# Nine of twelve modulation chunks multiplied and folded by GpSimd, with TensorE summing them over partitions

## What is computed

```python
mod = jax.nn.silu(c) @ w_ada[l] + b_ada[l]              # c: 1 x 1024, w_ada: 1024 x 6144
sh1, sc1, g1, sh2, sc2, g2 = jnp.split(mod, N_MOD, axis=-1)
h = layer_norm(x) * (1.0 + sc1[:, None]) + sh1[:, None]
x = layer_norm(ALPHA * x + g1[:, None] * mix, ln1_g[l], ln1_b[l])
```

## Time and profile before

| | |
|---|---|
| median of 3 runs | 2429.97 us (2426.4 to 2431.11) |
| the profiled execution | 2420.81 us, span 2418.7 us |
| TensorE busy | 2067.4 us (85%) |
| VectorE busy | 1560.9 us (65%) |
| ScalarE busy | 1184.9 us (49%) |
| GpSimd busy | 809.6 us (33%) |
| mean granted clock of TensorE | 0.91 |
| chain that ended last | TensorE 50%, DMA 24%, VectorE 12%, ScalarE 7%, issue 5%, GpSimd 3% |

### The profile page before, as it was taken

The page is one execution under the profiler, slowest core; times in us unless marked ns, Lnnn a source line. Parts: engine busy times, 40 slices in busy tenths (PEclk is TensorE's granted clock), DMA queues, the critical chain, the costliest instruction groups (busy, mean ns, idle before and its releaser), DMA issues.

```text
span 2418.7 us, 34343 instructions
## 1 busy us (share of the span) xinstructions
PE 2067.4 (85%) x13020; PEld 1579.0 (65%) x13020; DVE 1560.9 (65%) x3481; ACT 1184.9 (49%) x2367; POOL 809.6 (33%) x684
## 2 busy tenths in 40 slices
PE   6989998887697886666669899787998899989998
PEld 4445576776555555555567788656887657858863
DVE  5565665698875677788566776567766536854422
ACT  1123332466556667666676567756776740111110
POOL 2000000465743334455544896323433320700000
PEclk9999889999798998666679999988999999999999
DMA  4321235788899999999999999999999986353431
GB/s 170 122 96 70 72 139 210 284 325 315 336 366 410 414 418 415 420 421 421 418 416 415 402 356 416 415 417 412 413 413 411 411 311 226 114 191 108 171 139 70
DMA packets 162132, 729.71 MB, mean 302 GB/s; under 512 B 10160, under 2 KB 13360, under 8 KB 95920
## 3 DMA queue, kind: packets, MB, share of 16 engines
q0 software_dynamic: 73728, 536.90, 55.0%
q1 hardware_dynamic: 88240, 190.62, 21.7%
HBM read 725.38 MB, written 2.10 MB: 301 GB/s over the span
## 4 chain that ended last, share of the span: by engine, by line
PE 50%; DMA 24%; DVE 12%; ACT 7%; issue 5%; POOL 3%; SPq 0%; DVEq 0%; POOLq 0%; ACTq 0%
DMA AR<-in_uv,C 19%; PE PA L925 14%; PE PD L1514 8%; PE PA L1444 5%; PE PD L925 5%; PE PA L1457 3%; ACT AR L2032 3%; DMA WR<-in_w_up 2%; DMA WR<-in_w_down 2%; DVE AR L2892 2%; PE PA L1598 2%; PE PD L1598 2%; PE PA L1283 1%; PE PA L1296 1%; PE PA L1391 1%
## 5 line engine op out<-in xcount | busy, mean ns | idle before, releaser
L2892 DVE CUSTOM_DVE_ANT_0 AR<-AR,HN 128x1024 f32<-128x1024 f32 x467 | 591.6, 1271 | 366.3 <-issue 192.7
L3186 POOL DMA_INDIRECT AR<-in_uv,C x467 | 573.9, 1229 | 725.1 <-PE PD L1514 672.1
L1514 PE MATMUL PD<-C,AR 128*128 128x128 f32 x3736 | 586.7, 310 | 222.4 <-ACT AR L2032 220.7
L1514 PEld LDWEIGHTS PD<-C,AR 128*128 128x128 f32 x3736 | 497.7, 160 | 351.6 <-ACT AR L2032 301.5
L2032 ACT ACTIVATE AR<-AR,SC 128x1024 f32<-128x1024 f32 x467 | 536.6, 1149 | 15.2
L2028 ACT ACTIVATE SC<-SC 128x1 f32<-128x1 f32 x512 | 103.5, 202 | 406.9 <-DVE SC L2892 406.1
L3186 POOL DMA_INDIRECT WR<-in_uv,C x45 | 54.0, 1200 | 464.0 <-DVE C L2640 394.4
L1444 PE MATMUL PA<-HT,WR 128*128 128x256 f32 x704 | 167.6, 385 | 9.5 <-DMA WR<-in_w_up 9.5
L925 PE MATMUL PA<-HT,WR 128*128 128x256 f32 (+1 forms) x544 | 170.9, 475 | 0.0
L925 PE MATMUL PA<-AR,WR 128*128 128x256 f32 (+1 forms) x896 | 170.0, 352 | 0.7 <-ACT AR L1817 0.7
L925 PEld LDWEIGHTS PA<-AR,WR 128*128 128x128 f32 x896 | 152.2, 193 | 17.7 <-ACT AR L1817 1.1
(11 more groups left out here) (495 smaller groups left out, 3085.3 us busy)
## 6 DMA issues: line engine op xcount, KB each, us to landing
WR<-in_w_up SPq DMA_DIRECT2D x22, 2048.0 KB, 15.6
WR<-in_w_in SPq DMA_DIRECT2D x18, 2048.0 KB, 12.5
WR<-in_w_ada SPq DMA_DIRECT2D x12, 2048.0 KB, 8.1
WR<-in_w_down SPq DMA_DIRECT2D x9, 2048.0 KB, 9.2
WR<-in_w_pq SPq DMA_DIRECT2D x8, 2048.0 KB, 18.8
WR<-in_w_o SPq DMA_DIRECT2D x4, 2048.0 KB, 18.4
WR<-in_w_out SPq DMA_DIRECT2D x4, 2048.0 KB, 19.0
AR<-in_uv,C POOLq DMA_INDIRECT x467, 14.6
```

The lines of the kernel that those rows point to most:

```text
L1514: ins = nc.tensor.matmul(acc[i // 4][:, P * (i % 4):P * (i % 4) + P], uv_row(j, D + P * i, D + P * i + P), ident, start=(k == 0 and i % 4 ...
L2892: ttr(uv_row(j, 0, D), uv_row(j, 0, D), HN[:, t, :], 1.0, 0.0, ALU.mult, ALU.add, DOT[:, j:j + 1]).then_inc(s["dots"], 1)
L3186: nc.gpsimd.indirect_dma_start(uv_row(ring_slot(turn), 0, 2 * D), None, uv, bass.IndirectOffsetOnAxis(ap=IDX[:, t % 2, i:i + 1], axis=0),) ...
```

## The change

Chunks 3 to 11 leave TensorE's `modulation_rows`. GpSimd waits for each chunk's load, multiplies it in place with `csil2` (repeated over the 512 columns), folds its 8 blocks to 4, 2 and 1 by three sums, the last into `ADAROW[i]`, and counts `ada`. TensorE's `modulation_columns(i)` waits for `ada` and sums over all 128 partitions by a column of ones, again 4 products. Columns of chunks 2, 3 and 4 stand where rows 3 and 4 were, those of 5 to 8 together after the second `head_sums`, ahead of `rhat`; 9, 10 and 11 stay. `ADAROW` gets places in X for chunks 3 to 8. The nine chunks alternate between slots 0 and 1, each load waiting for GpSimd's last sum on that slot; the halves of `w_o` use slots 2 and 1. `down_part` gives 8 steps in 3 rows in place of 3 a row, and the turn of `xn3` goes ahead of the first `in2` products.

```diff
+def down_part(row):
+    at = [min(max(8 * (row + i - DOWN_FROM) // 3, 0), DOWN_IN_ROWS) for i in (0, 1)]
+    return range(at[0], at[1])
...
-        ADAROW = [HN[:, 2 + i % 2, 512:1024] for i in range(12)]
+        ADAROW = ([HN[:, 2 + i % 2, 512:1024] for i in range(3)]
+                  + [X[:, i // 2, 512 * (i % 2):512 * (i % 2) + 512] for i in range(6)]
+                  + [HN[:, i, 512:1024] for i in range(1, 4)])
...
-            col_chunk(w_ada, 512 * i, 512, "a", ada_job(i))
-        SLOTS += [0, 1, 0, 1, 2, 0, 1, 2, 0]
-        col_chunk(w_o, 0, 512, "d", FIRST_D[("wo", 0)])
-        col_chunk(w_o, 512, 512, "a", FIRST_A[("last", 7)])
+            col_chunk(w_ada, 512 * i, 512, "ada", i - 3)
+        SLOTS += [0, 1, 0, 1, 0, 1, 0, 1, 0]
+        col_chunk(w_o, 0, 512, "a", FIRST_A[("last", 7)])
+        col_chunk(w_o, 512, 512, "d", FIRST_D[("wo", 0)] + 1)
...
-        SLOTS += [1, 2, 0, 3, 1, 0, 1]
+        SLOTS += [2, 1, 0, 3, 1, 0, 1]
...
+                    elif chan == "ada":
+                        sp.wait_ge(s["ada"], job + 1)
...
-                pe.wait_ge(s["a_free"], ada_job(i) + 1)
+                if i < 3:
+                    pe.wait_ge(s["a_free"], ada_job(i) + 1)
+                else:
+                    pe.wait_ge(s["ada"], i - 2)
                 b = bank("a")
                 for m in range(4):
-                    ins = nc.tensor.matmul(b[:, m:m + 1], ADAROW[i][:, P * m:P * m + P], cc("sel")[:, 0:1],
+                    ins = nc.tensor.matmul(b[:, m:m + 1], ADAROW[i][:, P * m:P * m + P],
+                                           cc("sel" if i < 3 else "ones")[:, 0:1],
                                            start=True, stop=True)
...
-            for i in (3, 4):
-                modulation_rows(i)
-                modulation_columns(i - 1)
+            for i in (2, 3, 4):
+                modulation_columns(i)
...
             head_sums()
-            modulation_columns(4)
+            for i in range(5, 9):
+                modulation_columns(i)
             pe.wait_ge(s["rhat"], 2)
...
-                if lev > 1:
-                    modulation_columns(lev + 3)
...
-                modulation_rows(lev + 4)
...
-            modulation_rows(10)
             modulation_columns(10)
-            modulation_rows(11)
...
-                for c in part(r, DOWN_FROM, 3, DOWN_IN_ROWS):
+                for c in down_part(r):
...
+            turn_block("xn3", 3, "dd")
             pe.wait_ge(s["a_free"], FIRST_A["xn3_2"] + 2)
...
-            turn_block("xn3", 3, "dd")
             pe.wait_ge(s["d_free"], FIRST_D["in2"])
...
+            pool.wait_ge(s["cleared"], 1)
+            pool.wait_ge(s["csil"], 1)
+            for i in range(3, 12):
+                number = CNUM["ada3"] + i - 3
+                pool.wait_ge(w_sem[SLOTS[number]], 16 * (len(EARLIER[number]) + 1))
+                z = HOME[SLOTS[number]].rearrange("p (k n) -> p k n", k=KD)
+                joined(tt_(z, z, csil2.unsqueeze(2).broadcast_to([P, KD, 512]), ALU.mult), "mod")
+                joined(tt_(z[:, 0:4, :], z[:, 0:4, :], z[:, 4:8, :], ALU.add), "mod")
+                joined(tt_(z[:, 0:2, :], z[:, 0:2, :], z[:, 2:4, :], ALU.add), "mod")
+                if i >= 9:
+                    pool.wait_ge(s["a_full"], FIRST_A["ada0"] + 1)
+                joined(tt_(ADAROW[i], z[:, 0, :], z[:, 1, :], ALU.add), "ada")
```

More of the change, by code:

```diff
@@ L180 @@
     ("hT", 4, 4), ("pm", 4, 4), ("ada_pm", 1, 0), ("cT", 3, 2), ("q", 4, 4), ("kv", 4, 4), ("qkT", 16, 8), ("ada_qk", 2, 0),
-    ("att", 38, 64), ("pr", 2, 0), ("ada0", 4, 0), ("lora", 12, 0), ("tok", 4, 0), ("ada1", 1, 0), ("kn", 0, 5), ("bonus", 0, 1),
+    ("att", 38, 64), ("pr", 2, 0), ("ada0", 3, 0), ("lora", 12, 0), ("tok", 4, 0), ("ada1", 4, 0), ("kn", 0, 5), ("bonus", 0, 1),
 ]:
@@ L194 @@
         jobs("a", ("mt", _lev))
-    if _lev > 1:
-        jobs("a", ("columns", _lev + 3))
     jobs("d", ("right", _lev, 0), 2)
@@ L204 @@
         jobs("a", ("kk", 0))
-    jobs("a", ("rows", _lev + 4))
 jobs("a", ("left", LEVELS - 1, 0))
@@ L211 @@
 jobs("d", ("state", 0))
-jobs("a", ("rows", 10))
 jobs("a", ("columns", 10))
-jobs("a", ("rows", 11))
 for _c in range(1, NT):
@@ L386, in ada_job @@
 def ada_job(i):
-    if i >= 5:
-        return FIRST_A[("rows", i)]
-    return (FIRST_A["ada_pm"], FIRST_A["qkT"] + 6, FIRST_A["ada_qk"], FIRST_A["ada0"], FIRST_A["ada0"] + 2)[i]
+    return (FIRST_A["ada_pm"], FIRST_A["qkT"] + 6, FIRST_A["ada_qk"])[i]
 def in2_job(b):
@@ L498, in build @@
                  "xn", "xn2", "xn3", "xn4",
-                 "row_half", "ct_b", "ct_p", "e_full", "e_free", "mats", "ynorm", "ycomb_p", "cn", "qk_normed", "masked", "smax", "probs", "raw_used", "lora_in", "prt",
+                 "ada", "mod", "row_half", "ct_b", "ct_p", "e_full", "e_free", "mats", "ynorm", "ycomb_p", "cn", "qk_normed", "masked", "smax", "probs", "raw_used", "lora_in", "prt",
                  "kx_sq", "kr", "rkk", "rexp", "rhat", "khat", "cleared",
@@ L943, in modulation_rows @@
             def modulation_rows(i):
-                w = chunk(pe, CNUM["ada0"] if i == 0 else CNUM["ada1"] + i - 1 if i < 3 else CNUM["ada3"] + i - 3)
+                w = chunk(pe, CNUM["ada0"] if i == 0 else CNUM["ada1"] + i - 1)
                 b = bank("a")
```

## The result

| | before | after |
|---|---|---|
| median of 4 runs each, same chip | 2428.18 us (2423.57 to 2431.11) | 2506.62 us (2498.27 to 2507.68) |
| profiled execution, span | 2420.81, 2418.7 us | 2506.52, 2504.1 us |
| first gather | 428.81 us | 502.51 us |
| GpSimd busy | 809.6 us | 956.7 us |
| TensorE busy, mean granted clock | 2067.4 us, 0.91 | 2070.7 us, 0.89 |

The ratio is 1.0319, 95% interval 1.0295 to 1.0344: 78 us slower.

A forecast was written before the change was run, and what follows sets the result against it. Prologue to the first gather bounds the kernel, TensorE leading from 320 us, but VectorE's earlier stretch decides this change: 80 - 9.4 + 2 - 2.9 = +70 us, profiled 2491, forecast 2500 on the runs' median; range 2445 to 2520.

The forecast's parts named there:

- The hold of VectorE: From the last mix at 263 us, VectorE's SBUF operations take turns with GpSimd's whole instructions: 80 us later.
- no turn at all: Bound where VectorE stands until GpSimd ends at 357 us, then works alone: 94 late, less 6, so 88 us.
- GpSimd's prices: Per chunk on GpSimd: product 7.1 us, sums 4.6, 2.38 and 1.28, with joins 15.7 us; nine chunks 141 us.
- Attention: Attention's VectorE steps read PSUM or are one element wide, so should be nearly free of the hold.
- the third rival: Attention's one-element operations are held too by chunks 4 and 5: up to +20, 2519 us; inside the forecast's 0.70.
- Columns 5 to 8 together: Four column products on TensorE ahead of `rhat`: cost 0 to 3.3 us, taken as 2.
- The levels: Rows and columns taken from TensorE in the level stretch, from the first `left` to `y`: 9.4 us gained.
- Rows of chunks 10 and 11: Removing them from TensorE gives nothing, since the first turned tile waits for VectorE's output norm, ending at 388.1 us.
- The end: Turn of the last tile ahead of the first `in2` products, so the second ones start earlier: 2.9 us gained.
- The `down` steps and the `w_o` halves: Spreading 76 `down` steps over 28.5 rows: nothing, give or take 1 us; swapping the `w_o` halves: nothing.
- Rival 1: GpSimd's work hides and VectorE loses under 10 us: 2430 - 14 = 2416 us; chance 0.13.
- rival 2: VectorE wins every meeting, GpSimd delays `rhat` about 30 us: +20, 2450; chance 0.13 including what lies between it and forecast.

The follow-up runs named there:

- the version with four chunks: Before, with GpSimd taking only chunks 3 to 6, TensorE keeping chunks 7 to 11, and the turn of the last normed tile moved: 2438.5 us, ratio 1.0044.
- second filler run: After, with 11 useless products spread over four groups of 32 output partitions ahead of the columns of chunk 10, and again of chunk 11: 2496.8 us, ratio 1.0303.
- the extra GpSimd work: Before, with 25 two-input GpSimd operations added on idle space from near 231 us, and one late VectorE wait for their end: 2458.7 us, ratio 1.0134.
- both versions: The version with four chunks (2438.5 us), and before with GpSimd taking only chunks 3 and 4 after a wait for attention's mixes (2421.5 us, ratio 0.9985).
- both filler runs: After with useless products ahead of the columns of chunks 10 and 11: all in one group of output partitions 2506.5 us, spread over four 2496.8 us.

## Why the prediction was right, step by step

The forecast was 2500 and 2506.6 came; the mechanism was the forecast one. Up to the first gather the sum was 80 + 2 - 9.4 = 72.6, and 73.7 was measured. That the two are so close is in part luck, since several terms were off and cancel:

- **The hold of VectorE: 80 taken (81 by the walk), 74.1 in the trace,** of which 2.6 are already there at 150 us, ahead of anything that differs. So the term was some 8.5 us too large. The step that failed is "VectorE gets one instruction or a short run at a time": it gets exactly one. I let GpSimd pay for nearly all of VectorE's 23 us; VectorE got only 24 instructions in, and they cost GpSimd 0.3 us or less each. GpSimd's last 24 instructions took 95.3 us and ended at 360.7, not 380, and VectorE's remaining 13.6 us came behind. The bound that I had named for "no turn at all" (88) has the same form, and lay on the other side.
- **GpSimd's prices held.** The product took 7.02 us (7.1 forecast), the sums 4.50, 2.34 and 1.26 (4.6, 2.38, 1.28). The Trainium skill's single price (GPSIMD Engine Reference, "Performance versus the Vector engine"), by which I had estimated 8.9 us for the product, doesn't hold for a factor repeated along the inner dimension. Chunk 4 started at 234.4 (231.5), 5 at 249.9, 6 at 265.4, and GpSimd never waited for a load from there.
- **Attention** was free, as forecast, but for a reason that I had only half: its PSUM and one-element operations are free, its mixes are not, and only one of them met GpSimd in after (2.29 and 4.88 us for its two instructions). In the version with four chunks attention does suffer, as the third rival had it, but through the mixes and the clock, not through the one-element operations.
- **Columns 5 to 8 together: 3.2 us** (from `rhat` to the first `x1`); 2 was taken, 3.3 the upper bound. Ahead of it a term was missing: TensorE had stood 41 us for VectorE, its first 64 instructions behind that (L1077) took 5.90 us instead of 3.71, and the delay grew by 1.1 us up to `rhat`.
- **The levels: 9.4 forecast, 9.3 measured** to the last sum of level 5 (delay 78.4 at the first `x1`, 69.05 there; 10.0 up to `left` of level 6).
- **Rows of chunks 10 and 11 "give nothing": they cost.** The way from the output norm to the first gather grew by 4.5 us. The products taken away were what TensorE did while it waited for VectorE. Without them it stood 3.75 us and then ran a part of the `w_o` products at the lower clock. The second filler run gave back 3 of the 4.5 in its trace.
- **The end: -2.9 forecast.** The two products of `in2` adjoin as named, 3.3 us earlier against the last row's turn, but the constants' load and VectorE's chain took over. From that turn to the end it is 416.75 us in after, 418.46 in before, and 416.7 in the run with only the `down` steps moved, so what differs there can't be told from chance. Alone, the turn gave nothing. The prediction had not asked what else ends just behind.
- **The `down` steps and the `w_o` halves at nothing:** the first may cost a few us, the second can't be told from nothing.
- **The rows.** From the first gather to the last row's turn it is 1571.4 us in before and 1584.8 in after, 13.4 us that the sum didn't have. Four kernels with little or nothing changed there (the turn alone, the extra GpSimd work, both versions) have 1574.9 to 1578.3, so some 3 to 7 of these are the good profiled execution of before; 3.2 are the first four gathers. The code of the rows can't be behind all of the rest: the run without GpSimd's long operations and the second filler run execute exactly after's rows and took 1577.4 and 1577.6, so 7 of the 13.4 us come and go between executions of the same rows. What makes them is open.

Rival 1 (hidden) fell with the extra work in before, rival 2 (VectorE first) with the two traces: it was VectorE that stood. The named signs came: GpSimd busy without a break from 234 to 361 us, the means of 3 to 5 us, the shapes that read PSUM unchanged (L2280, in before L2283, 284 ns in both). One named sign failed: L2320 to L2322 kept their own times, since GpSimd was through before them.

## What to carry to other kernels

Before work goes to an idle GpSimd, list what VectorE does in that stretch: every VectorE instruction with two SBUF inputs, and every tensor_scalar or copy within SBUF, costs it the rest of the GpSimd instruction that it meets, one for one. Put long GpSimd instructions where VectorE reads PSUM or stands still; where they must overlap, cut them short, even if they get dearer in sum. And before work is taken from an engine that waits anyway, look at whether it was keeping TensorE's clock up.

## What the runs showed of the hardware

- GpSimd on fp32: with a factor repeated along the inner dimension 4096 elements took 7.02 us (1.7 ns each), a plain sum of 2048 4.50 us (2.2), a multiplication by a constant 10.55 us for 4096 (2.6), a memset 3.55 us for 4096 (0.87). The one-input form is the dearest.
- The hold is exclusive and goes by whole instructions for two-input operations. Beside the one-input form VectorE's held instruction ended 1.2 us before the recorded end of GpSimd's (273.90 and 275.08 us); GpSimd's recorded spans are rough.
- Eleven products of 384 columns on 32 output partitions took 7.3 us when all went to one group of partitions, and 2.1 us when spread over four.
- The 32 instructions of the `w_o` products took 14.00 us with TensorE busy ahead of them (before and both filler runs), and 16.4 to 16.6 after it had stood 3.7 us (after, and the run without GpSimd's long operations).
- The granted clock can fall without a change of the kernel: from 230 to 260 us it was 1.00 in before, and 0.65, 0.50 and 0.82 in an execution with the same prologue, which was 10 us later at the mixes behind.
